# Retention output products of heads 0 to 2 as pairs of 64 rows on the two row halves of the array

## What is computed

```python
def retention_mixer(h, pos, w_in, w_out):
    q, k, v, z = _split(h @ w_in, ODD_SPLITS)
    q = xpos_rotate(q.reshape(qk_shape), pos)
    k = xpos_rotate(k.reshape(qk_shape), pos) * (RET_QK_DIM ** -0.5)
    o = rms_norm(multiscale_retention(q, k, v)).reshape(bsz, s, ODD_MIX)
    return (jax.nn.silu(z) * o) @ w_out
```

## Time and profile before

| | us |
|---|---|
| median of 3 runs | 1672.25 (1671.3 to 1672.84) |
| profiled execution, its own time | 1674.15 |
| its span, first to last instruction | 1672.1 |
| TensorE (PE) busy | 1640.6 |
| VectorE (DVE) busy | 679.7 |
| ScalarE (ACT) busy | 411.9 |
| GpSimd (POOL) busy | 226.1 |

### The profile page before, as it was taken

How to read it: one execution, slowest core, us unless ns; L and a number is a source line. 1 busy time by engine, 2 the same in 40 slices (tenths; PEclk the granted TensorE clock), 3 DMA queues, 4 the chain that set the end, 5 groups by cost and what they waited for, 6 DMA issues and landing times.

```text
span 1672.1 us, 22392 instructions
## 1 busy us (share of the span) xinstructions
PE 1640.6 (98%) x9377; PEld 1055.1 (63%) x9377; DVE 679.7 (41%) x1238; ACT 411.9 (25%) x766; POOL 226.1 (14%) x162
## 2 busy tenths in 40 slices
PE   7999899999999999999999999999999999999997
PEld 7878788745445454547888888888754544445443
DVE  4887763533423243334413223242623333324333
ACT  4576663300000000004332414223500000000000
POOL 1600101000000000003444344432100000000000
PEclk9999999999999999999999999999999999999999
DMA  9420222899999999997313122223699999999995
GB/s 207 106 51 1 66 90 101 345 420 425 423 427 427 425 427 423 426 424 271 105 51 101 65 87 101 92 82 143 265 389 424 427 423 427 426 425 425 426 426 230
DMA packets 79383, 460.86 MB, mean 276 GB/s; under 512 B 6960, under 2 KB 32784, under 8 KB 53552
## 3 DMA queue, kind: packets, MB, share of 16 engines
q1 hardware_dynamic: 78544, 457.03, 67.5%
q0 software_dynamic: 736, 2.34, 1.2%
HBM read 457.25 MB, written 2.10 MB: 275 GB/s over the span
## 4 chain that ended last, share of the span: by engine, by line
PE 93%; DVE 2%; DMA 2%; ACT 2%; issue 1%; SPq 0%; DVEq 0%; ACTq 0%
PE bank L161 31%; PE bank L1958 26%; PE bank L1978 13%; PE bank L1985 7%; PE bank L1916 7%; DMA ring<-in_w_up_dram 1%; PE bank L1969 1%; PE bank L1622 1%; DMA ring<-in_w_in_even_dram 0%; PE bank L1909 0%; PE bank L2542 0%; PE bank L2655 0%; PE bank L1610 0%; PE bank L1032 0%; PE bank L1941 0%
## 5 line engine op out<-in xcount | busy, mean ns | idle before, releaser
L1958 PE MATMUL bank<-ring,SCR 128*64 128x512 f32 x1760 | 445.9, 592 | 1.5 <-issue 1.0
L161 PE MATMUL bank<-ring_r 128*128 128x512 f32 (+2 forms) x1120 | 337.5, 380 | 1.5 <-DVE ring_r L445 1.5
L1958 PEld LDWEIGHTS bank<-ring,SCR 128*64 128x64 f32 x1760 | 146.3, 137 | 245.5 <-issue 245.0
L161 PEld LDWEIGHTS bank<-ring_r 128*128 128x128 f32 x1120 | 206.1, 188 | 41.2 <-issue 2.9
L1978 PE MATMUL bank<-ring,SCR 128*64 128x512 f32 x880 | 226.7, 595 | 0.0
L1950 DVE SCALAR_TENSOR_TENSOR X<-bank,AU,X 128x512 f32<-128x512 f32 x256 | 173.7, 744 | 88.9 <-PE bank L1985 88.9
L1997 DVE TENSOR_TENSOR SCR<-SCR,bank 128x512 f32<-128x512 f32 x32 | 22.0, 688 | 361.8 <-PE bank L1958 361.8
L1978 PEld LDWEIGHTS bank<-ring,SCR 128*64 128x64 f32 x880 | 70.1, 137 | 121.3 <-issue 121.3
L161 PE MATMUL bank<-ring_r,SCR_r 128*128 128x512 f32 x576 | 138.5, 395 | 0.0
L2511 POOL TENSOR_TENSOR ring_r<-ring,ring_r 128x1024 fp32r<-128x1024 f32 x48 | 117.0, 2470 | 143.9 <-ACT ring_r L2497 143.9
L1985 PE MATMUL bank<-SCR_r 128*128 128x512 f32 x512 | 131.9, 400 | 0.3 <-DVE SCR_r L1994 0.3
(11 more groups left out here) (463 smaller groups left out, 1884.3 us busy)
## 6 DMA issues: line engine op xcount, KB each, us to landing
ring<-in_w_gate_dram SPq DMA_DIRECT2D x53, 2048.0 KB, 16.5
ring<-in_w_down_dram SPq DMA_DIRECT2D x51, 2048.0 KB, 15.9
ring<-in_w_up_dram SPq DMA_DIRECT2D x50, 2048.0 KB, 19.6
ring<-in_w_in_odd_dram SPq DMA_DIRECT2D x8, 2048.0 KB, 9.2
SCR<-in_w_up_dram SPq DMA_DIRECT2D x10, 1024.0 KB, 15.5
SCR<-in_w_gate_dram SPq DMA_DIRECT2D x9, 1024.0 KB, 12.3
SCR<-in_w_down_dram SPq DMA_DIRECT2D x9, 1024.0 KB, 18.3
ring<-in_w_in_even_dram SPq DMA_DIRECT2D x16, 512.0 KB, 6.5
```

The costliest lines, as they stand in the source:

```text
L161: mm = pe.matmul(out, lhs[a], rhs[b], start=(first and i == 0), stop=(last and i == 2))
L1958: mm = pe.matmul(bank[SLOTS * u:SLOTS * u + SLOTS, :], xt[:, k, SLOTS * u:SLOTS * u + SLOTS], w[u](k), start=(k == 0), stop=(k == KT - 1))
```

## The change

Heads 0 to 2 make the output products with `split_rows_mm`: each matmul over 128 rows becomes two over rows 0 to 63 and 64 to 127, which go to two different banks, 24 matmuls a product. The products go in turn to banks 4 and 5 and to banks 6 and 7, and VectorE adds both banks, one behind the other. Since banks 6 and 7 are the transposes' banks, all four tiles are transposed ahead of the products: tiles 2 and 3 now stand between the two products of the second QK half. The first product waits for the last Z activation (bank 5 free), the second for all four subtractions of the transposes (banks 6 and 7 free). Head 3 stays as it was.

```diff
--- before.py
+++ after.py
@@ -159,6 +159,14 @@
 
             for i, (a, b) in enumerate(((0, 0), (0, 1), (1, 0))):
                 mm = pe.matmul(out, lhs[a], rhs[b], start=(first and i == 0), stop=(last and i == 2))
+            return mm
+
+        def split_rows_mm(pe, outs, lhs, rhs, first, last):
+
+            for i, (a, b) in enumerate(((0, 0), (0, 1), (1, 0))):
+                for r, out in enumerate(outs):
+                    rows = slice(64 * r, 64 * r + 64)
+                    mm = pe.matmul(out, lhs[a][rows], rhs[b][rows], start=(first and i == 0), stop=(last and i == 2))
             return mm
 
         class Carve:
@@ -2562,6 +2570,8 @@
                 for t in between if s else ():
                     ret_yt_pe(pe, h - 1, t)
                 for par in range(2):
+                    for t in (2, 3) if s + par == 2 and between else ():
+                        ret_yt_pe(pe, h - 1, t)
                     if h:
                         pe.wait_ge(sg("r_o_out"), NT * (h - 1) + 2 * s + par + 1)
                     for k in range(KT):
@@ -2614,10 +2624,7 @@
                         ret_z_pe(pe, h, t)
                     ret_qk_pe(pe, h + 1, (0, 1))
                     for n in range(8):
-                        if n == 2:
-                            ret_yt_pe(pe, h, 2)
-                            ret_yt_pe(pe, h, 3)
-                        ret_out_pe(pe, h, n)
+                        ret_out_rows_pe(pe, h, n)
                 else:
                     ret_z_pe(pe, h, 1)
                     ret_z_pe(pe, h, 2)
@@ -2671,6 +2678,28 @@
                     pe.wait_ge(sg("r_lower"), 4 * i + j + 1)
                 mm = split_mm(pe, PB[4 + n % 2][:, :], [a[:, t, j, :] for a in (YTr, YTl)],
                               [a[:, j, half * 512:(half + 1) * 512] for a in w], j == 0, j == 3)
+            mm.then_inc(sg("r_out"), 1)
+
+        def out_rows(n):
+
+            return PB[4 + 2 * (n % 2)], PB[5 + 2 * (n % 2)]
+
+        def ret_out_rows_pe(pe, h, n):
+            i, c, w = odd_chunk("out", h)
+            w = [a.rearrange("p (k n) -> p k n", k=4) for a in w]
+            t, half = n // 2, n % 2
+            if n == 0:
+                pe.wait_ge(sg("r_zs"), NT * h + NT)
+            elif n == 1:
+                pe.wait_ge(sg("r_ytl"), NT * h + NT)
+            else:
+                pe.wait_ge(resid, R_MOE0 + 8 * h + n - 1)
+            pe.wait_ge(sg("r_ytl"), NT * h + t + 1)
+            for j in range(4):
+                if n == 0:
+                    pe.wait_ge(sg("r_lower"), 4 * i + j + 1)
+                mm = split_rows_mm(pe, [b[:, :] for b in out_rows(n)], [a[:, t, j, :] for a in (YTr, YTl)],
+                                   [a[:, j, half * 512:(half + 1) * 512] for a in w], j == 0, j == 3)
             mm.then_inc(sg("r_out"), 1)
 
         def ret_act(act, step):
@@ -2790,17 +2819,18 @@
                         yt_lower(h, 0)
                 if h < RH - 1:
                     rotate(h + 1, both[0:1])
-                for t in range(2) if h < RH - 1 else range(1, 3):
+                for t in range(NT) if h < RH - 1 else range(1, 3):
                     yt_lower(h, t)
                 for n in range(8):
                     t, half = n // 2, n % 2
-                    if h < RH - 1 and n == 2:
-                        yt_lower(h, 2)
-                        yt_lower(h, 3)
                     dve.wait_ge(sg("r_out"), 8 * h + n + 1)
                     xs = X[:, t, half * 512:(half + 1) * 512]
                     dve.wait_ge(resid, R_MOE0 + 8 * h)
-                    dve.tensor_tensor(xs, xs, PB[4 + n % 2][:, :], ALU.add).then_inc(resid, 1)
+                    if h < RH - 1:
+                        step.then(dve.tensor_tensor(xs, xs, out_rows(n)[0][:, :], ALU.add))
+                        dve.tensor_tensor(xs, xs, out_rows(n)[1][:, :], ALU.add).then_inc(resid, 1)
+                    else:
+                        dve.tensor_tensor(xs, xs, PB[4 + n % 2][:, :], ALU.add).then_inc(resid, 1)
                     if h == RH - 1:
                         if n == 0:
                             yt_lower(h, 3)
```

## The result

The changed kernel takes 1686.67 us (median of 4 runs, 1685.36 to 1688.28) against 1672.01 us for the kernel before beside it: a ratio of 1.0088, 95% interval 1.007 to 1.0105, or 14.7 us more. The profiled execution took 1685.36 us.

A forecast was written before the change was run, and what follows sets the result against it. TensorE, busy 98% of the span, was taken as the bound. To 1672.25 us were added 8.4 (2.8 per head, three heads) and 3 x 1.5 for the clock: +12.9, 1685.2 us, range 1678.5 to 1690.5.

The forecast's parts named there:

- The wait: Second output product of heads 0 to 2: TensorE idles some 3.4 us until ScalarE's casts and copies and VectorE's subtractions end.
- The moved transposes: Second half of the QK products: 0.96 us of transposes move there without a wait; nothing is added.
- The pairs: Output products: 0.216 us per pair instead of 0.227 per matmul, at most 1.04 us gained per head.
- the attention's row: Profile row of 16 f32 matmuls, 64x256, on alternating row halves in 2.00 us; gave 0.216 us per step.
- The sum for one head: Wait, seven pair products and leaving the row mode, clock at full: +2.8 us per head, +8.4 for three.
- Entering and leaving: TensorE's row mode: leaving costs 0.2 us per head; entering about as much, hidden at the first product.
- VectorE's second add: 24 more adds of 0.69 us; about 1.4 us per product against 2.59 for a pair product, so hidden.
- The clock: Behind each wait the granted clock halves for 3.4 us, costing 1.5 us per head, bounds 0 and 1.7.
- the wait without the clock: Rival: the wait comes but the clock stays at 1.00 behind it; +8.4, 1680.7 us; chance 0.27.
- The wait met in time: Rival: subtractions end before the first product does, leaving the pairs' gain; -1.9, 1670.3 us; chance 0.05.
- Lack of overlap: Rival: fp32r halves do not run beside each other; +22.8 us per head, 1741 us; chance 0.05.
- loads in the open: Rival: 0.19 us of each 0.227 is a load only row pairs hide; -12.2 per head, 1635.6 us; chance 0.01.

The follow-up runs named there:

- the probe: Copies ahead of casts, products for 256 of 512 columns in heads 0 to 2: f32 steps 0.216 us on row halves and full rows, fp32r pairs 0.121.
- the filled kernel: The changed kernel with three full-array f32 matmuls of 512 columns, read by nothing, issued while the second product waits: 1683.94 us, ratio 1.006.
- the reordered kernel: The changed kernel with ScalarE making all four transpose copies ahead of the casts of the next head's V weights: 1675.05 us, ratio 1.0011.
- the three filled profiles: Unread matmuls in the wait: six in the changed kernel, 1690.08 us; three in it, 1683.94; three with the wait but 128-row matmuls, 1682.47.

## Why the prediction was right, and which terms were off

Forecast 1685.2 us, measured 1686.67, inside the range. By its own steps:

- **The wait.** Right in cause and place, and nearly in size. Forecast: first product issued at 884.5, subtractions done at 887.81 (885.87 + 1.91 is 887.78), second product at 887.96, so some 3.4 us. Measured: last pair of the first product started at 884.7, and the next could have followed 0.227 later, at 884.9; subtractions done at 887.89, second product at 887.94, so 3.0 us, in a trace that runs 0.17 us later at this place. Undoing it alone gives back 3.2 us per head.
- **The moved transposes** cost nothing by themselves, as forecast: 99.75 us per head without wait and pairs.
- **The pairs** are the term that was mis-sized. I took 0.216 us per pair from the attention's row and named 0.227 as the bound "if the remainder belongs to the fp32r operand". That is what the probe shows. The row was the nearest by its rows (halves) and not by its operand (f32); the rows of the same operand, fp32r matmuls at 0.227, were the better ones. That "no row tells apart" the operand and the full rows was a reading error, too. The expert layer in the trace of before has f32 matmuls (no `_r` in their operands' names) over all 128 rows, in pairs of 64 weight columns; of each pair, the first:

```profile
508.85 0.59 PE L1978 MATMUL bank<-ring,SCR 128*64 128x512 f32 x1
...
509.28 0.59 PE L1978 MATMUL bank<-ring,SCR 128*64 128x512 f32 x1
...
509.71 0.59 PE L1978 MATMUL bank<-ring,SCR 128*64 128x512 f32 x1
...
510.14 0.59 PE L1978 MATMUL bank<-ring,SCR 128*64 128x512 f32 x1
```

A step is 0.43 us for 512 columns, twice the 0.216 of the attention's 256 columns and not twice 0.227 (0.454): f32 on all rows lacks the remainder. The sum for one head goes from +2.8 to +3.7 us, the value that I had worked out for the bound, and 103.4 - 99.75 confirms it.

- **Entering and leaving**: 0.2 each. In the kernel without the wait, 0.49 us per head in all.
- **VectorE's second add** is hidden, as forecast: no wait of TensorE for it, in any kernel.
- **The clock** falls behind waits, but not behind each one: behind one of three in one profile and two of three in the other. A fall costs 1.6 us, forecast 1.5; that it comes behind each wait was wrong. Of the measured 14.7 us, 3 x 3.7 = 11.0 are wait and row mode (the filled kernel, without a fall in its profile, took 1683.94 - 1672.6 = 11.3 more than before), and 3.7 are left for the clock, by estimate some 2.3 falls. The filled wait takes 2.3 us away, some 1.5 falls. I had 8.4 and 4.5, so the pairs' error and the clock's partly cancelled; that 1685.2 came so close is in part luck.

The rivals: the wait without the clock is what a part of the heads did. The wait met in time is what the reordered kernel made of it, at 1675 and not 1670, since its gain had the pairs' error in it. Lack of overlap is refuted, as a pair takes what a full matmul took. So are loads in the open: pairs on two row halves run no faster (0.227 us) than one full array that reloads each time (0.227). The Trainium skill (TensorE: Matmul & The Clock Gate, The mechanism) says that a weight load overlaps with matmuls in flight only when the row groups differ; in this kernel's traces that does not hold. The same section also has loads into a background weight buffer pulled ahead; no run here shows whether that is how these loads are hidden.

No version here beats the kernel before. With the loss removed entirely it is that kernel's time again.

## What to carry to other kernels

When a change makes two uses share a buffer, follow the release of the shared buffer back through every in-order queue: here the place of two lines on an engine that was 75% idle cost TensorE 3.2 us a head, because the copies that free the banks stand behind casts that nothing needed yet. Before splitting a matmul over row halves, ask what the full matmul wastes: here weight loads were hidden already and all 128 rows were used, so halves brought nothing and cost the entry, the exit and a second add. And price an operation by a row with the same operand type before one with the same shape.

## What the runs showed of the hardware that was not expected

- fp32r matmuls take about 0.014 us more than their columns' time at 2.4 GHz, on full rows and on row halves, at 512 columns (0.227) and at 256 (0.120 to 0.121); f32 in the same places takes 0.216 per 256-column step. The Trainium skill (TensorE: Matmul & The Clock Gate, Back-to-back issue gap) gives the columns' time at 2.4 GHz plus 2.5 ns for what it calls the isolated gap of a matmul, which for 512 columns is 0.216 us. The f32 rows agree with it, taken (an estimate) as two passes over their 256 columns; the fp32r rows do not. For a stream of loads and matmuls the same section gives about 131 ns at 512 columns; no stream on the full array here comes near that (0.227).
- An f32 matmul shows as two matmuls in the trace: one of 512 columns takes 2 x 0.43 us.
- Some 3 us of idle time (2.87) in the middle of dense matmuls were followed by 3.4 us at the 1.2 GHz level in three of six cases with row pairs. Where the idle time was 3.12 us, with 128-row matmuls, the level fell in three of three, in two of them for 6.8 us that began in the idle time. Filling the wait with matmuls that nobody reads removed it in all nine waits of the three filled profiles.
- Going over to row halves and back each cost TensorE 0.2 us: the step onto the first pair is 0.32 us and the next 0.34, instead of 0.227, and the same again onto the full rows.
